# First eight products and the values of sixteen heads with tokens as stationary operand and 512 weight columns moving

## What is computed

```python
def gmlp_shortconv_mixer(h, w_in, w_s, b_s, conv_w, w_out):
    proj = h @ w_in
    a_u, a_v, g_b, g_c, b_x = jnp.split(
        proj, [A_WIDTH, 2 * A_WIDTH, 2 * A_WIDTH + B_WIDTH, 2 * A_WIDTH + 2 * B_WIDTH], axis=-1)
    a_u = jax.nn.gelu(a_u)
    a_v = jax.nn.gelu(a_v)
    ...                                    # a_v is normed over its 1024 features, mixed over tokens
def dilated_attention_mixer(h, w_qkv, w_o, positions):
    qkv = h @ w_qkv
    q, k, v = jnp.split(qkv, 3, axis=-1)   # 16 heads of 128
    q = rope(q.reshape(bsz, s, ATTN_HEADS, ATTN_HEAD_DIM), positions)
    k = rope(k.reshape(bsz, s, ATTN_HEADS, ATTN_HEAD_DIM), positions)
    ...                                    # softmax(q k) v per head, then @ w_o
h = h + rmsnorm(mix, norm_mix_post[layer])
f = squared_relu_mlp(rmsnorm(h, norm_mlp_pre[layer]), w_up[layer], w_down[layer])
h = h + rmsnorm(f, norm_mlp_post[layer])
```

## Time and profile before

| | |
|---|---|
| median of 3 runs | 3078.92 us (3078.68 to 3080.38) |
| the profiled execution | 3076.82 us, of which the span from first to last instruction 3074.9 us |
| mean granted TensorE clock, as a share of full speed | 0.993 |
| busy: TensorE, its weight loads | 3028.6 us (98%), 2665.7 us (87%) |
| busy: VectorE, ScalarE, GpSimd | 2182.8, 1463.7, 281.9 us |
| bytes moved | 548.29 MB, mean 178 GB/s |

### The profile page before, as it was taken

The page is one execution under the profiler, slowest core; times in us unless marked ns, Lnnn a source line. Parts: engine busy times, 40 slices in busy tenths (PEclk is TensorE's granted clock), DMA queues, the critical chain, the costliest instruction groups (busy, mean ns, idle before and its releaser), DMA issues. The chain is left out here.

```text
span 3074.9 us, 48189 instructions
## 1 busy us (share of the span) xinstructions
PE 3028.6 (98%) x17775; PEld 2665.7 (87%) x17775; DVE 2182.8 (71%) x2911; ACT 1463.7 (48%) x1845; POOL 281.9 (9%) x191
## 2 busy tenths in 40 slices
PE   8999999999999999999999999999999999999999
PEld 7888888888888888888888888888888888888888
DVE  6777775767666687765856666676788865879764
ACT  5334544433334554545533334344656645656544
POOL 0002300000000400004100000002300004200003
PEclk9999999999999999999999999999999999999999
DMA  6555455555555444445455554555444445344445
GB/s 239 181 187 188 168 188 185 188 191 191 188 186 188 163 168 175 165 152 205 172 186 189 191 191 177 196 188 190 156 162 176 151 150 184 149 179 155 157 150 191
DMA packets 77131, 548.29 MB, mean 178 GB/s; under 512 B 8544, under 2 KB 9056, under 8 KB 11232
## 3 DMA queue, kind: packets, MB, share of 16 engines
q1 hardware_dynamic: 77024, 546.81, 49.0%
HBM read 544.68 MB, written 2.10 MB: 178 GB/s over the span
## 5 line engine op out<-in xcount | busy, mean ns | idle before, releaser
L838 ACT ACTIVATE w_high<-raw 128x2048 fp32r<-128x2048 f32 x511 | 975.2, 1908 | 1107.6 <-DMA raw<-stream 1106.9
L307 PE MATMUL acc<-xs,w_high 128*128 128x512 f32 x4947 | 1244.2, 396 | 9.6 <-ACT w_high L978 8.7
L1257 DVE TENSOR_TENSOR w_low<-raw,w_high 128x2048 fp32r<-128x2048 f32 x511 | 1164.9, 2280 | 106.9 <-ACT w_high L838 103.7
L307 PEld LDWEIGHTS acc<-xs,w_high 128*128 128x128 f32 x4947 | 911.4, 189 | 196.5 <-ACT w_high L978 8.7
L307 PE MATMUL acc<-inner,w_high 128*128 128x512 f32 x2880 | 692.2, 391 | 0.0
L314 PE MATMUL acc<-xs,w_low 128*128 128x256 f32 x4962 | 685.8, 284 | 0.0
L314 PEld LDWEIGHTS acc<-xs,w_low 128*128 128x128 f32 x4962 | 657.9, 192 | 23.3
L1266 DVE TENSOR_REDUCE y<-acc 128x256 f32<-128x512 f32 x406 | 279.8, 690 | 483.1 <-PE acc L314 478.1
L307 PEld LDWEIGHTS acc<-inner,w_high 128*128 128x128 f32 x2880 | 528.2, 188 | 101.9 <-issue 0.7
L314 PEld LDWEIGHTS acc<-inner,w_low 128*128 128x128 f32 x2976 | 382.2, 191 | 15.0
L314 PE MATMUL acc<-inner,w_low 128*128 128x256 f32 x2976 | 386.8, 282 | 0.0
(11 more groups left out here) (188 smaller groups left out, 1423.4 us busy)
## 6 DMA issues: line engine op xcount, KB each, us to landing
raw<-stream SPq DMA_DIRECT2D x514, 1024.0 KB, 4.8
h<-x_t SPq DMA_DIRECT2D x4, 512.0 KB, 7.6
out<-finished SPq DMA_DIRECT2D x8, 256.0 KB, 2.1
raw<-stream SPq DMA_DIRECT2D x2, 512.0 KB, 6.8
consts<-tables SPq DMA_DIRECT2D x1, 960.0 KB, 16.2
branch<-w_spatial SPq DMA_DIRECT2D x1, 512.0 KB, 17.0
branch<-b_spatial SPq DMA_DIRECT2D x1, 512.0 KB, 17.8
prob_t<-lambdas SPq DMA_DIRECT2D x1, 256.0 KB, 17.8
```

Of the source, the lines that this page charges most:

```text
L307: nc.tensor.matmul(acc[s][:, :], w_high[:, s, kt * P:(kt + 1) * P], x[:, kt, :, :], start=(kt == first_of[0]), stop=False, skip_group_chec ...
L838: nc.scalar.activation(w_high[:, s, 0:units * P], raw[:, s, 0:units * P], ACT.Copy)\
L1257: V.tensor_tensor(w_low[:, s, 0:units * P], raw[:, s, 0:units * P], w_high[:, s, 0:units * P], ALU.subtract).then_inc(low_ready, 1)
```

## The change

It has two places. In each, groups of four chunks are laid out anew: chunk i of a group holds rows 512 i to 512 i + 511 of four times 128 weight columns, as four 128x512 blocks. The tokens become the stationary operand (128 tokens of one feature block, high or low part) and 512 weight columns move. A chunk adds to two PSUM banks, one for each half of the tokens; after four chunks the banks hold 512 output features with tokens on partitions.

The first place is products 0 to 7 (two groups, banks 0, 1 and 2, 3). x comes in five pieces and chunk i waits only for its x blocks. ScalarE squares x after the fifth chunk's high part, VectorE sums the squares after that chunk's low part; the sums go into product 6 and the spread into product 7. GELU reads the banks, scales by `root_of` per partition and writes `a_v`; the transposes, the scalings and the sums of halves are gone.

The second is the values: the stream is now, per four heads, four chunks of v and then q and k of each head. ScalarE copies the two banks, scaled, to `v_four`. The banks of the q and k products are shifted by two in every other group (`off`). The scores of a head now stand after the next head's q product, the turn of its probabilities after that head's k product, the weighing one product later; for the last head of a group they stand between the wide products of the next group, and for head 15 in the output stage. The loop of three iterations is written out.

```diff
+            def wide_high(c, i, s, x, bank, units=range(KT_WIDE), high=None, xs_base=None, hooks=None,
+                          parts=(0, 1)):
+                pe.wait_ge(*(high or (high_ready, c + 1)))
+                for a in units:
+                    kt = KT_WIDE * i + a
+                    if hooks and a in hooks:
+                        hooks[a]()
+                    for part in parts:
+                        if xs_base is not None:
+                            pe.wait_ge(sem("xs_ready" if part else "xs_high"), xs_base + kt + 1)
+                        for n in range(TB):
+                            mm = nc.tensor.matmul(acc[bank + n][:, :], x[:, kt, part, n * P:(n + 1) * P],
+                                                  w_high[:, s, a * WIDE:(a + 1) * WIDE],
+                                                  start=(kt == 0 and part == 0), stop=False, skip_group_check=True)
+            def wide_low(c, i, s, x, bank, units=range(KT_WIDE), low=None):
+                pe.wait_ge(*(low or (low_ready, c + 1)))
+                for a in units:
+                    kt = KT_WIDE * i + a
+                    for n in range(TB):
+                        mm = nc.tensor.matmul(acc[bank + n][:, :], x[:, kt, 0, n * P:(n + 1) * P],
+                                              w_low[:, s, a * WIDE:(a + 1) * WIDE], start=False, stop=(kt == KB - 1),
+                                              skip_group_check=True)
...
+            wide_high(0, 0, 0, xs, 0, units=(0, 1), high=(sem("first_high"), 1), xs_base=0)
+            wide_low(0, 0, 0, xs, 0, units=(0, 1), low=(sem("first_low"), 1))
+            wide_high(0, 0, 0, xs, 0, units=(2, 3), xs_base=0)
+            wide_low(0, 0, 0, xs, 0, units=(2, 3)).then_inc(product_done, 1)
+            for i in range(1, 4):
+                wide_product(i, i, i, xs, 0, xs_base=0)
+            wide_product(4, 0, 0, xs, 2)
+            wide_product(5, 1, 1, xs, 2)
+            wide_product(6, 2, 2, xs, 2, hooks={0: stat_of_input})
+            wide_product(7, 3, 3, xs, 2, hooks={1: lambda: spread(0)})
...
+            for i in range(HEADS // 4):
+                c, off = C_QKV + 12 * i, 2 - 2 * (i % 2)
+                before = 4 * i - 1
+                if i == 0:
+                    wide_first(c, 2, 2 - off, hooks={0: lambda: stat_pre(2, 2)})
+                    spread(4)
+                else:
+                    pe.wait_ge(summed, c - 2)
+                    for j in range(4):
+                        wide_product(c + j, j, j, xs, 2 - off)
+                        if j == 0:
+                            dilated_scores(before)
+                            dilated_weigh(before - 1)
+                        if j == 1:
+                            turn_prob(before, before % 2)
+                        if j == 2:
+                            dilated_weigh(before)
                 for g in range(4):
+                    hd, cq, s = 4 * i + g, c + 4 + 2 * g, 2 * g % 4
+                    if g == 1:
+                        pe.wait_ge(sem("v_four_ready"), TB * i + TB)
+                    product(cq, s, xs, bank=(s + off) % 4)
+                    if g > 0:
+                        dilated_scores(hd - 1)
+                    if g > 1:
+                        dilated_weigh(hd - 2)
+                    product(cq + 1, s + 1, xs, bank=(s + 1 + off) % 4)
+                    if g > 0:
+                        turn_prob(hd - 1, (hd - 1) % 2)
+            hd = HEADS - 1
+            out_section(C_OUT1, 80, 2, 2, hooks={
+                8: lambda: dilated_weigh(hd - 1), 20: lambda: dilated_scores(hd),
+                36: lambda: turn_prob(hd, hd % 2), 41: lambda: dilated_weigh(hd)})
...
+            for i, (a, b) in enumerate(INPUT_PIECES):      # (0,2) (2,4) (4,8) (8,12) (12,16)
+                act.wait_ge(sem(f"x_landed_{i}"), 16)
+                for kt in range(a, b):
+                    input_high(0, kt)
...
+                else:
+                    high(i - 1, i - 1)
+            ahead(1, 1)
             for part in range(2):
                 k = part * KB // 2
                 nc.scalar.activation(x_squares[:, k:k + KB // 2, :], h[:, k:k + KB // 2, :], ACT.Square)\
                     .then_inc(sem("squared"), KB // 2)
+            def gelu_av(g):
+                act.wait_ge(product_done, 4 * g + 4)
+                act.wait_ge(sem("root_ready"), 1)
+                for n in range(TB):
+                    nc.scalar.activation(a_v[:, n, g * WIDE:(g + 1) * WIDE], acc[2 * g + n][:, :], ACT.Gelu_apprx_tanh,
+                                         scale=root_of[:, n:n + 1]).then_inc(sem("av_copied"), 1)
+            for j in range(2, 5):
                 ahead(j, j % 4)
+            gelu_av(0)
+            for j in range(5, A_BLOCKS):
+                ahead(j, j % 4)
+            gelu_av(1)
```

More of the change, by code:

```diff
@@ L467, in turn_value, with weigh @@
                 mm.then_inc(sem("v_turned"), 1)
-            def weigh(u, bank, values, o, v=None, part=(0, P), count=1, last=True):
+            def weigh(u, bank, values, o, v=None, four=None, part=(0, P), count=1):
                 pe.wait_ge(sem("prob_t_ready"), u + count)
@@ L1068, in _, with copy_four @@
[L1068 to L1073 removed]
+            def copy_four(i, bank, r, done, free):
+                act.wait_ge(product_done, done)
+                act.wait_ge(sem("root_ready"), r + 1)
+                act.wait_ge(sem("head_done"), free)
+                for n in range(TB):
+                    nc.scalar.activation(v_four[:, n, :], acc[bank + n][:, :], ACT.Copy, scale=root_of[:, n:n + 1])\
+                        .then_inc(sem("v_four_ready"), 1)
@@ new lines, in no_sums, with four_chunks @@
+            def no_sums(c):
+                dve.wait_ge(summed, c)
+                V.tensor_copy(unused, minus_half[:, :]).then_inc(summed, 4)
+            def four_chunks(c, r, sd, copied, tables, done, count):
+                no_sums(c)
+                ahead(c + 1, 1)
+                mean(r, D, NORM_EPS, "stat_done", sd + 1)
+                ahead(c + 2, 2)
+                scale_out(r, copied, scale_pre[:, :])
+                scaled_tables(tables, rope_s, scale_pre[:, :], done, count)
+                ahead(c + 3, 3)
@@ L1907, in blocks, with wide @@
             put(w[:, first + width * i:first + width * (i + 1)])
+    def wide(w, first):
+        for i in range(4):
+            rows = w[i * WIDE:(i + 1) * WIDE, first:first + WIDE].reshape(KT_WIDE, P, WIDE)
+            stream[at[0]] = rows.transpose(1, 0, 2).reshape(P, UNITS, P)
+            at[0] += 1
     w = w_in_ab[0]
     width = A_BLOCKS * P
-    blocks(w, width, A_BLOCKS)
+    for first in range(width, 2 * width, WIDE):
+        wide(w, first)
     for j in range(A_BLOCKS):
@@ L1922, in weight_stream @@
     mlp(0)
-    for hd in range(HEADS):
-        for part in range(3):
-            blocks(w_qkv[0], D * part + P * hd)
+    for i in range(HEADS // 4):
+        wide(w_qkv[0], 2 * D + WIDE * i)
+        for hd in range(4 * i, 4 * i + 4):
+            for part in range(2):
+                blocks(w_qkv[0], D * part + P * hd)
     blocks(w_o[0], 0, KB)
```

331 lines of the change are left out of this document (143 added, 188 removed).

## The result

| | before | after |
|---|---|---|
| median, same chip | 3078.68 us (5 runs, 3077.34 to 3080.38) | 3062.59 us (5 runs, 3060.65 to 3064.13) |
| ratio | | 0.995, 95% interval 0.9938 to 0.9961 |
| profiled execution, its span | 3076.82, 3074.9 us | 3062.59, 3060.9 us |

A forecast was written before the change was run, and what follows sets the result against it. TensorE, busy 3028.6 of 3074.9 us, was taken as the bound. Start 9.2 us (with 0.2 for the mix) plus heads 7.0 made 16.2 off 3078.9: 3062.7 us; own range 3058 to 3067, with rivals 3056 to 3070.

The forecast's parts named there:

- The pitch: In the wide chunks, 512-column matmuls with weights moving start 0.228 us apart, so a chunk takes 5.47 us, not 5.56.
- The rivals of a dearer pitch: Wide chunks: pitch 0.239, 3069 us (6%); or slower than before, at 0.270 giving 3087 us (3%).
- The clock under two banks: Wide chunks: alternating PSUM banks costs nothing; the rival, half clock throughout these chunks, gave 3194 us (2%).
- The start: Products 0 to 8: product 9 starts at 62.4 instead of 71.38, a gain of 9.0 us.
- The wait of 2.0 us: Inside product 5, TensorE waits 2.0 us for VectorE's low part; a rival without this wait (10%) gave 3060.7 or little lower.
- The clock stays at 1.00 after it: After the wait in product 5 TensorE keeps full clock; half clock again would cost 1.6 us more.
- the mix: First mix after the start: its 0.2 us wait goes, because VectorE's variance chain is 1.2 us less late.
- The heads: The sixteen heads gain 7.0 us: transposes of v 3.7, wide chunks 1.4, rotated k 2.2, less 0.3.
- The 2.2 us of the rotated k: First head's neighbour: the 2.2 us wait for the rotated k goes, as scores come one product after their k.
- The 0.3 allowed for the output stage: Output stage: head 15's scores, turn and weighing follow closely, leaving an estimated wait of 0.3 us, between 0 and 1.
- The columns at half clock are as many: After the norm ahead of the heads the half-clock start stays, with as many columns at half clock as before.
- The rival of 0.4 us per head: Sixteen heads: a new wait in each from the softmax within two products, 6.4 us in all, giving 3069 us (12%).

The follow-up runs named there:

- the second profile of the same kernel: The changed kernel run again unaltered, on another chip than its first profile: 3060.12 us (5 runs), ratio 0.9943 to the kernel before.
- the first place alone: The kernel before with only products 0 to 7 and the start changed, the heads as before: 3073.32 us (10 runs), ratio 0.9985.
- the experiment: The changed kernel with two transposes of the identity put back in each of the sixteen turns of the probabilities: 3069.62 us, one run.

## Why the prediction was right, step by step

**The pitch** was right: 0.227 instead of 0.228. Matmuls on two banks in turn with 512 columns of weights moving cost what those with 512 columns of tokens cost on one bank. The small difference is worth 0.03 us per chunk. Over 16 chunks of values that is 1.9 us against 1.4 forecast. The rivals of a dearer pitch fell: at 0.239 a chunk would be 5.73 us.

**The clock under two banks** was right. In the stretch from 23.1 to 35.0, wide products throughout, the granted clock is 1.00. The Trainium skill, "TensorE: Matmul & The Clock Gate", section "A second HAM failure mode: psum-queue depth-cycling", had spoken against it; this trace shows no such fall.

**The start** was forecast at 9.0 us and gave 5.4 in the profile: the term that was mis-sized. Three of its steps were off. The 5.4 is one execution: in the second profile of the same kernel product 9 gains 4.3 us.
- The second chunk's weights were to be split at 14.9; ScalarE had them at 16.36, and TensorE stood 1.7 us for them. My steady rate of 418 GB/s was too high for the first microseconds (207 to 347 GB/s from 1.5 to 10 us). Product 1 ended at 21.97, 1.2 us later than forecast. This cost nothing in the end: TensorE came 1.0 us later to the wait in product 5, whose end the fifth weights set.
- The fifth weights were to start at 28.94 as before and started at 30.43, the low part of chunk 5 was ready at 44.5 and not at 42.9. The wait of 2.0 us was forecast at its place, by its mechanism, and is 2.5. I had named fifth weights later than 29 us as a sign of being wrong, and this sign came; why they came 1.5 us later behind the same bytes was not tried. The late start of the low matmuls, 44.58 instead of 42.9, is 1.7 of the missing 3.6 us, and the clock after it nearly all of the rest.
- "The clock stays at 1.00 after it" failed: 1.6 us in the low matmuls, 0.1 in the sums. I had judged by one row, the 2.2 us gap of the earlier trace rows. The same gap in the first place alone was followed by clock 0.50. Over the runs the wait in product 5 cost between 0.2 and 3.4 us on top of its length. The forecast's own range had this case in it at 1.6 us.

**Between product 9 and the heads** 0.2 us were forecast for the mix and 1.3 came. The wait of the mix is gone, and 0.5 us in all are gained by the end of the mix. Another 0.5 is a shorter wait for ScalarE's squares ahead of the norm, 1.53 us before and 1.04 after; over the profiles it lies between 0.90 and 2.22, so it is not to be put down to the change. The rest was not tried. The distance from product 9 to the norm varies from 991.8 to 994.5 us over the kernels, whose code there is the same.

**The heads** were forecast at 7.0 us and gave 8.1. Transposes: 3.7 forecast, 3.54 by the experiment. Wide chunks: 1.9 instead of 1.4. The 2.2 us of the rotated k: gone, as forecast. The 0.3 allowed for the output stage did not come up: none of its small operations waits. That is 7.6 to 7.8. "The columns at half clock are as many" did not hold in this execution: 1.55 us of clock are missing after the norm instead of 3.01. Of these 1.5 us the late root, which I had not foreseen, takes back about 1.1 (24.80 against 22.2 + 1.55), so 0.4 is left, which makes 8.0 to 8.2. In the second profile, with 2.95 missing, the gain is 7.9. The stage up to the output stage's first matmul was forecast at about 295 us and is 293.1. "No wait per head" was right: from the norm to the output stage the root is TensorE's only wait. The rival of 0.4 us per head fell; two-product heads follow one another every 12.8 to 12.9 us.

**The sum** came out within 0.1 us of the median, but not because each term did. By the profiles the terms were 3.6 too high at the start, 1.1 too low before the heads, 1.1 too low in them, and 0.8 were given back after them: 14.0 instead of 16.2. The missing 2.1 us are the distance of the profile before to its median, which I added to the forecast and which the profile after does not have. A second measurement of the changed kernel gave 16.9 us. Each of the two has an interval of some 4 us to either side; the agreement to 0.1 is luck.

## What to carry to other kernels

Swapping the stationary and the moving operand costs nothing in itself when columns, type and run length are kept; what it gains is what no longer has to be turned, and what later waits are moved. When a stall is taken away, follow what each feeding engine does in the time that has become free: here two engines stood idle for 6 us and then did the wanted work last, and moving one transfer was worth 4.4 us, as much as the whole first place; moving one block of code took the same wait away. A short wait of TensorE should be priced with both outcomes of the clock, since one row shows only one of them.

## What the runs showed of the hardware

- After a wait of TensorE of 2.2 to 2.8 us the granted clock may stay at 1.00 (2.4 GHz) or go to 0.50 (1.2 GHz), with the same code: the 2.2 us wait for k was followed by 1.00 in the kernel before and by 0.50 with the first place alone; after the wait in product 5 it was 1.00 with the first place alone (0.2 us lost), 0.52 for 3.4 us in the first profile of the changed kernel (1.7 us lost) and 0.50 from 46 to 52 in its second (3.3 us lost).
- After the same norm the clock missing in 12 us was 1.49 to 3.01 us over twelve profiles. A late operand further on can hide that difference fully, as the table of the root shows.
- A GpSimd operation on 128x2 values took 2.61 to 2.68 us beside VectorE's subtraction of 128x2048 values and 0.70 us without. The Trainium skill, "SBUF — State Buffer", section "SBUF: two separate sides", says that a VectorE operation with two SBUF inputs and a GpSimd operation that reads SBUF lock each other out of a shared pair of ports for a whole instruction. The trace agrees: GpSimd's operation, started 0.16 us after VectorE's, ended 0.6 us after VectorE's was over, and was back at 0.70 us when VectorE was held back.
